# An eight-core decoder step: a second u buffer, the layer-norm weight in PSUM and late gating matmuls in place of a bf16 start of FFN 0

## The reference, cut to what matters

```
layer 0: x += 0.5 * swiglu(rmsnorm(x));  x += even_mixer(rmsnorm(x));  x += 0.5 * swiglu(rmsnorm(x))
layer 1: x += 0.5 * swiglu(rmsnorm(x));  x += odd_mixer(rmsnorm(x));   x += 0.5 * swiglu(rmsnorm(x))
y = rmsnorm(x)
rmsnorm(x)   = x * rsqrt(mean(x*x) + 1e-6) * g
swiglu(h)    = (silu(h @ w_gate) * (h @ w_up)) @ w_down            # width 2816
even_mixer:  uv = gelu(h @ w_in[:, :1024]);  u = uv[:512]
             v  = layernorm(uv[512:]) * ln_g + ln_b
             y_a = u * (tril(w_s) . v + b_s)                       # per head, in chunks of 128 tokens
             y_b = gate_b * conv3(gate_c * x_in)                   # three more projections of h
             out = [y_a, y_b] @ w_out
```

## Time and profile before

| what | value |
|---|---|
| median of the runs | 2394.33 us |
| lowest run, which is the profiled one | 2394.22 us |
| its span, first to last instruction, slowest core (5) | 2392.7 us |
| spans of the eight cores | 2362.3 to 2392.7 us |
| TensorE busy | 2329.3 us, 97% |
| VectorE / ScalarE / GpSimd busy | 1014.0 / 546.3 / 216.3 us |

### The profile page before, as it was taken

The page is one execution under the profiler, slowest core; times in us unless marked ns, Lnnn a source line. Parts: engine busy times, 40 slices in busy tenths (PEclk is TensorE's granted clock), DMA queues, the critical chain, the costliest instruction groups (busy, mean ns, idle before and its releaser), DMA issues.

```text
span 2392.7 us, 33520 instructions; the slowest of 8 cores (2362.3 to 2392.7 us)
## 1 busy us (share of the span) xinstructions
PE 2329.3 (97%) x12456; PEld 1225.2 (51%) x12456; DVE 1014.0 (42%) x1717; ACT 546.3 (23%) x992; POOL 216.3 (9%) x261
## 2 busy tenths in 40 slices
PE   6999999998999999999999999999989999999996
PEld 3455555554555555555555555555544555555553
DVE  4752232276567242232382422322796624223226
ACT  4401101254234101101242011012433310110123
POOL 2100000165000000000000000001500000000014
PEclk9999999999999999999999999999998899999998
DMA  8052222210422132222220522222231113222203
GB/s 225 18 84 36 36 36 36 36 20 13 68 41 32 25 60 36 36 36 36 36 32 5 80 36 36 36 36 36 49 72 21 32 24 61 36 36 36 36 1 150
DMA packets 21326, 107.38 MB, mean 45 GB/s; under 512 B 4016, under 2 KB 6064, under 8 KB 11696
## 3 DMA queue, kind: packets, MB, share of 16 engines
q0 software_dynamic: 12528, 84.42, 22.5%
q1 hardware_dynamic: 8640, 20.82, 2.6%
HBM read 174.89 MB, written 11.08 MB: 78 GB/s over the span
## 4 chain that ended last, share of the span: by engine, by line
PE 91%; DVE 4%; issue 2%; ACT 1%; DMA 1%; POOL 1%; DVEq 0%; ACTq 0%; SPq 0%; POOLq 0%
PE ps L436 88%; PE ps L431 2%; DVE hT L665 1%; PE ps L724 1%; DVE scr L1153 0%; PE ps L608 0%; DVE xT L653 0%; DVE xT L820 0%; DMA ws<-wall 0%; DVE hT L653 0%; DVE misc L898 0%; POOL mid L948 0%; DMA xT<-x 0%; ACT scr L916 0%; DMA scr<-spl 0%
## 5 line engine op out<-in xcount | busy, mean ns | idle before, releaser
L436 PE MATMUL ps<-hT,ws 128*128 128x512 bf16 (+2 forms) x7520 | 1403.2, 350 | 3.0 <-ACT mid L1131 2.2
L436 PEld LDWEIGHTS ps<-hT,ws 128*128 128x128 bf16 x7520 | 738.2, 98 | 660.9 <-issue 38.8
L436 PE MATMUL ps<-mid,ws 128*128 128x512 bf16 (+2 forms) x4160 | 783.8, 351 | 0.0
L713 DVE TENSOR_TENSOR mid<-ps,scr 128x512 bf16<-128x512 f32 (+2 forms) x428 | 261.4, 611 | 921.3 <-PE ps L436 886.0
L436 PEld LDWEIGHTS ps<-mid,ws 128*128 128x128 bf16 x4160 | 408.2, 99 | 368.5 <-issue 34.1
L708 ACT ACTIVATE scr<-ps 128x512 f32<-128x512 f32 (+2 forms) x428 | 227.5, 532 | 1405.8 <-PE ps L436 1335.2
L820 DVE SCALAR_TENSOR_TENSOR xT<-ps,xT 128x512 f32<-128x512 f32 (+2 forms) x480 | 290.0, 611 | 284.2 <-PE ps L436 283.6
L386 POOL DMA_DIRECT2D ws<-wall x83 | 44.4, 535 | 1954.3 <-PE ps L436 1936.4
L665 DVE SCALAR_TENSOR_TENSOR hT<-xT,misc,nrm 128x512 bf16<-128x512 f32 (+2 forms) x144 | 91.6, 677 | 4.4 <-ACT nrm L635 4.4
L431 PE MATMUL ps<-hT,ws 128*128 128x512 bf16 (+2 forms) x288 | 60.6, 365 | 2.9 <-DVE hT L665 2.9
L1061 DVE TENSOR_TENSOR xT<-ps,xT 128x512 f32<-128x512 f32 (+2 forms) x80 | 48.6, 610 | 34.6 <-PE ps L436 33.4
(11 more groups left out here) (108 smaller groups left out, 644.7 us busy)
## 6 DMA issues: line engine op xcount, KB each, us to landing
ws<-wall POOLq DMA_DIRECT2D x65, 1024.0 KB, 9.5
ws<-wall POOLq DMA_DIRECT2D x12, 768.0 KB, 8.9
y<-xT SPq DMA_DIRECT2D x4, 1024.0 KB, 3.9
xT<-x SPq DMA_DIRECT2D x6, 512.0 KB, 7.0
ws<-wall POOLq DMA_DIRECT2D x6, 512.0 KB, 16.8
xT<-x POOLq DMA_DIRECT2D x2, 1024.0 KB, 24.0
xT<-x SPq DMA_DIRECT2D x2, 1024.0 KB, 8.1
y<-xT SPq DMA_DIRECT2D x4, 512.0 KB, 2.7
```

What stands on the lines that cost most here:

```text
L436: ins = e.matmul(banks[bk][:, 0:n], l, rr, start=(i == 0), stop=(i == len(pairs) - 1))
L713: P.add("dve", lambda e: e.tensor_tensor(out=mcol(fs, a, a + n), in0=banks[ku][:, 0:n], in1=s_(0, n), op=ALU.mult), r=[("ps", ku), s_.key( ...
```

## The change

The bf16 start goes: `start`, `raw`, `raw_out`, `raw_in`, `direct`, `quad`, `line`, `rs0` and `finish_h`. Block 0 is normed chunk by chunk (eight groups; chunks 1, 3 and 6 of h by GpSimd and ScalarE), all its h are listed, and the cells start with block 0; block 1's norm is listed after the third cell, with its ones-matmul ahead of the fourth. x comes in 1 MB pieces on SyncE's queue: block 0 at once, block 1 after the second half of the first weight item, each later one after the block before. The six weight pieces follow each other on GpSimd's queue. Blocks 1 and 2 change sizes, to 512 and 384.

In the even mixer u has two buffers, by turns; `lngb` is copied by ScalarE into bank 7 once block 1 begins, after all h of the last block, and `center` reads it there from then on; the last two `sgu` stand behind the three groups of the first convolution cell, and so do the memset of `ext` and the state's DMA. The `xin` buffers move to the norm's scratch.

```diff
-BL = [(0, 512), (512, 384), (896, 512), (1408, 512), (1920, 256)]
-XPER = [2, 4, 4, 4, 4]
+BL = [(0, 512), (512, 512), (1024, 384), (1408, 512), (1920, 256)]
...
-    uT = R.f32(6 * T * 2, 4 * 512)
+    uTs = [R.f32(6 * T * 2, 4 * 512), NRM.f32(0, 4 * 512)]
...
-    xin = [SC.f32(2048 * i, 512) for i in range(2)]
+    xin = [NRM.f32(8192 + 2048 * i, 512) for i in range(2)]
...
-        for lo, hi in [part] if part else [(0, n)]:
+        pieces = [(0, 2048), (2048, 4096)] if j < 3 else [(0, n)]
+        for lo, hi in pieces:
...
                 P.label = "v norm"
-                P.add("dve", lambda e: e.scalar_tensor_tensor(out=g(0, 512), in0=g(0, 512), scalar=mv(2 * i, 2 * i + 1), in1=lngb(0, 512),
+                gain, gk = (banks[7][:], ("rsp",)) if gain7 else (lngb(0, 512), lngb.key(0, 512))
+                P.add("dve", lambda e: e.scalar_tensor_tensor(out=g(0, 512), in0=g(0, 512), scalar=mv(2 * i, 2 * i + 1), in1=gain,
...
             ensure_h(b)
+            if b == 1:
+                ensure_h(NB - 1)
+                P.label = "v norm"
+                P.add("act", lambda e: e.activation(out=banks[7][:], in_=lngb(0, 512), func=AF.Copy), r=[lngb.key(0, 512)], w=[("ps", 7), ("rsp",)])
+                gain7.append(1)
...
+            uT = uTs[b % 2]
             for j in range(4):
...
             prev = [(i, b) for i in tiles]
-        while prev:
-            sgu(*prev.pop(0))
         release(jv)
         release(ju)
...
                     mm_group(bk, n, [(wt(o + c * 128, o + c * 128 + 128), hs(b, c)) for c in range(NCH)],
                              [hk(b, c) for c in range(NCH)] + [wt.key(o, o + 1024)])
+                while prev:
+                    sgu(*prev.pop(0))
...
+                if cn["k"] == 1:
+                    P.add("sp", lambda e: [e.dma_start(out=exs(0, 640), in_=sc_in)], w=[exs.key(0, 640)], ndma=1)
+                    P.add("dve", lambda e: e.memset(ext(0, 2), 0.0), w=[ext.key(0, 2)])
...
-    for c in range(0, NCH, 2):
-        load_x("sp", 0, c)
-    load_item(0, (0, 2048), [xT.key(0, 1)])
-    load_item(0, (2048, 4096))
-    load_item(1, (0, 2048))
-    load_x("pool", 1, 0)
-    load_x("pool", 1, 4)
-    load_item(1, (2048, 4096))
-    load_x("pool", 2, 0)
-    load_x("pool", 2, 4)
-    load_item(2, (0, 2048))
-    load_item(2, (2048, 4096))
...
+    load_item(0, after=[xT.key(0, 1)])
+    load_item(1)
+    load_item(2)
+    for b in range(1, NB):
+        gate = wv(0).key(2048, 4096) if b == 1 else xT.key(xoff(b - 1, 4), xoff(b - 1, 4) + 1)
         for c in (0, 4):
-            load_x("sp", b, c, [gate])
+            load_x(b, c, [gate])
     nm0 = Norm(0)
+    nm0.groups[0] = 8
+    nm0.split[0] = (1, 3, 6)
+    nm0.pair_wait = 2
...
-        nm0.wait = 5
+        nm0.wait = 3 if b < 2 else 5
...
+    norm0(0)
+    ensure_h(0)
...
-    cells = [(2, 0, 3), first(3)] + [(2, f, 3) for f in range(1, 5)] + [finish_h(0), (2, 5, 3), first(4), lambda: load_item(3)] \
-        + [(3, f, 3) for f in range(4)] + [finish_h(1)] + [(3, f, 3) for f in range(4, 6)] + [(4, f, 3) for f in range(6)] + [even_consts, odd_consts]
+    cells = [(0, 0), (0, 1), (0, 2), first(1), (0, 3, 8), (1, 0), first(2), (1, 1), (1, 2), (1, 3), (0, 4), (1, 4),
+             first(3), (2, 0), (2, 1), (2, 2), (2, 3), (2, 4), (0, 5), (1, 5), (2, 5), first(4), lambda: load_item(3),
+             (3, 0), (3, 1), (3, 2), (3, 3), (3, 4), (3, 5)] + [(4, f) for f in range(6)] + [even_consts, odd_consts]
```

More of the change, by code:

```diff
@@ L317, in xdram @@
     def xdram(b, c0, c1):
-        return dram(x_in, b, c0, c1, XPER[b])
+        return dram(x_in, b, c0, c1, 4)
     def ydram(b, c0, c1):
@@ L368, in build_program, with load_item @@
     slot_of = {}
-    def load_item(j, part=None, after=()):
+    def load_item(j, after=()):
         key, n = ITEMS[j]
@@ L538, in heavy_chunk @@
             if i == end:
[L539 to L579, removed]
+                at(2 if alone else 5, lambda: self.stat(b, k, 0, 2 if alone else 1))
         def prescale(self, b, c):
@@ L594, in flush, with stat @@
                 self.scaled = None
-        def stat(self, b, k, gi, groups=None, own=False):
+        def stat(self, b, k, gi, groups=None):
             n = BL[b][1]
             bk, rk = 7, ("rsp",)
-            if own:
+            if groups == 2:
                 if gi == 0:
@@ L611, in stat @@
                 return
[L612 to L619, removed]
+            k2 = pc["rs"] % 2
+            pc["rs"] += 1
+            q = rs[k2]
+            while any(x[2] == k2 for x in hq):
+                hq.pop(0)[1]()
             P.label = f"norm{self.nidx} rs"
@@ L714, in gu @@
                   r=[("ps", ku), s_.key(0, n)], w=[mkey(fs, a, a + n)])
[L716 to L803, removed]
-                tick(3)
-                if b * 10 + f in (3, 12):
-                    for c in range(0, 4) if f == 3 else range(4, 8):
-                        nm0.line(2, c)
-            o[2]()
@@ L835, in ffn @@
                 js = [item(("gu", l, w, f)) for f in fs]
-                js0.extend(js)
-                if cells is not None:
-                    start()
                 if cells is None:
@@ L967, in even @@
                          [hk(b, c) for c in range(NCH)] + [wu_.key(j * 1024, j * 1024 + 1024)])
-                P.add("act", lambda e, j=j, bk=bk, n=n: e.activation(out=uT(j * 512, j * 512 + n), in_=banks[bk][:, 0:n], func=AF.Gelu),
+                P.add("act", lambda e, j=j, bk=bk, n=n, uT=uT: e.activation(out=uT(j * 512, j * 512 + n), in_=banks[bk][:, 0:n], func=AF.Gelu),
                       r=[("ps", bk)], w=[uT.key(j * 512, j * 512 + n)])
@@ L978, in even @@
         P.label = "conv init"
-        P.add("dve", lambda e: e.memset(ext(0, 2), 0.0), w=[ext.key(0, 2)])
-        P.add("sp", lambda e: [e.dma_start(out=exs(0, 640), in_=sc_in)], w=[exs.key(0, 640)], ndma=1)
         cn = dict(k=0)
@@ L1222, in build_program, with load_x, norm0 @@
     P.add("act", lambda e: e.activation(out=junk(0, 1), in_=mh(0, 1), func=AF.Square), r=[("mh",)], w=[("junk",)])
-    def load_x(eng, b, c, gate=()):
-        o0, o1 = xoff(b, c), xoff(b, c) + XPER[b] * BL[b][1]
+    def load_x(b, c, gate=()):
+        o0, o1 = xoff(b, c), xoff(b, c) + 4 * BL[b][1]
         P.label = "load x"
-        P.add(eng, lambda e: [e.dma_start(out=xT(o0, o1), in_=xdram(b, c, c + XPER[b]))], r=list(gate), w=[xT.key(o0, o1)], ndma=1)
+        P.add("sp", lambda e: [e.dma_start(out=xT(o0, o1), in_=xdram(b, c, c + 4))], r=list(gate), w=[xT.key(o0, o1)], ndma=1)
+    load_x(0, 0)
+    load_x(0, 4)
     P.label = "const"
     P.add("sp", lambda e: [e.dma_start(out=cT(0, 76), in_=cst)], w=[("cT",)], ndma=1)
-    for c in range(0, NCH, 2):
-        load_x("sp", 0, c)
-    load_item(0, (0, 2048), [xT.key(0, 1)])
-    load_item(0, (2048, 4096))
-    load_item(1, (0, 2048))
-    load_x("pool", 1, 0)
-    load_x("pool", 1, 4)
-    load_item(1, (2048, 4096))
-    load_x("pool", 2, 0)
-    load_x("pool", 2, 4)
-    load_item(2, (0, 2048))
-    load_item(2, (2048, 4096))
-    for b in range(3, NB):
-        gate = wv(2).key(0, 2048) if b == 3 else xT.key(xoff(b - 1, 4), xoff(b - 1, 4) + 1)
+    load_item(0, after=[xT.key(0, 1)])
[3 more added lines that the diff above has]
+        gate = wv(0).key(2048, 4096) if b == 1 else xT.key(xoff(b - 1, 4), xoff(b - 1, 4) + 1)
         for c in (0, 4):
-            load_x("sp", b, c, [gate])
+            load_x(b, c, [gate])
     nm0 = Norm(0)
+    nm0.groups[0] = 8
+    nm0.split[0] = (1, 3, 6)
+    nm0.pair_wait = 2
     cur_norm[0] = nm0
-    def nm0_block(b):
-        nm0.wait = 5
+    def norm0(b):
+        nm0.wait = 3 if b < 2 else 5
         for c in range(NCH):
@@ L1370, in to_blocks @@
     x3 = xt.reshape(NCH, 128, T)
-    return np.concatenate([x3[c:c + p, :, a:a + n].transpose(1, 0, 2).reshape(-1) for (a, n), p in zip(BL, XPER) for c in range(0, NCH, p)])
+    return np.concatenate([x3[c:c + 4, :, a:a + n].transpose(1, 0, 2).reshape(-1) for a, n in BL for c in (0, 4)])
 def from_blocks(y):
```

15 lines of the change are left out of this document (5 added, 10 removed).

## The result

The changed kernel takes 2367.28 us, the one before took 2394.27 beside it: ratio 0.9891, interval [0.9869, 0.9914]. That is 27 us faster where 8 were forecast; the time lies in the range of the prediction (2356 to 2399) and outside the likeliest case's own (2379 to 2392). Left out of every comparison and count here, unless one is named, are the runs in which one die took over 1% longer than the other at a lower clock, or which took over 1.5% longer than the fastest of their kernel.

The account below looks back on a forecast made before the run. TensorE, busy 2329 of 2392.7 us, was taken as the bound, with core 5 setting the time. From 2394.2, 7.8 us for gating and 0.5 for the start gave 2385.9, say 2386; range 2356 to 2399.

Parts of the forecast that it names:

- the likeliest case: Whole kernel: both edits win as summed and the slow stretch stays; 2386 us, own range 2379 to 2392, chance 0.58.
- Gating, what goes: Gating stage: TensorE's 5.9 us of waits and 1.9 us of half clock vanish; 7.8 us, bounds 4.8 to 7.8.
- Gating, what is added: Gating stage: centring from PSUM at 0.69 us, copy to PSUM, moved memset and DMAs; all put at nothing.
- The bank named as next to be late: Second convolution cell's third bank: freed 2 us after the gating matmuls, TensorE comes to it after 3.5 us.
- The clock: Gating stage: with no pause, granted clock stays 1.00 through its end, saving 1.9 us.
- Start, steps 1 to 4: Start: block 0's x, first weights, block 0's norm and cells 1 and 2, ending at 32.7 us.
- Step 3's rule: Block 0's norm: shared port fully blocking would make the h 7.6 us, not 5.7, and the start 1.9 us later.
- Step 5: Start, block 1's norm: TensorE waits from 32.7 to 39.7 us for VectorE's seven adds.
- the third case: Block 1's x behind the weights: lands at 37.6, ones-matmul at 41.7 us; part of the late-start rival, 2390 us, chance 0.13.
- The stretch: Core 5 at clock 0.81 from 1780 to 1940 us: not edited, so taken to stay, change nothing.
- The other rival: The 0.81 stretch grows as the load gets denser; twice as long gives 2416 us; chance 0.08.
- the rival of the lost stretch: Core 5 keeps its clock after 1780 us and gains 28 us: 2358 us; chance 0.10.

Follow-up runs that it names:

- e4: Kernel before (old bf16 start) with the new gating stage and the sample's v stored from its own tile; 2359.9 us without the stretch.
- e3: Changed kernel with the sample's v stored from a tile of its own; 2359.7, 2360.2 and 2360.6 us without the stretch.
- e12: e3 with the last gating matmuls ahead of the convolution matmuls again; first down matmul to end 2232.3 to 2234.0 us on spared cores.
- e10: e3 with one u buffer again; first down matmul to end 2229.1 to 2230.0 us on spared cores.
- e6: e3 with five more VectorE passes ahead of the first convolution product, an equal delay on every core; 2367.76 us.
- e2: Changed kernel with the gating stage of the kernel before; ratio 0.9943, 2368.2 to 2369.7 us without the stretch.
- e5: Changed kernel run again unaltered, on a chip without the stretch; 2367.36 us, ratio 0.9993.
- e9: Changed kernel run a third time unaltered, on a chip that shows the stretch; ratio 0.9928.
- e8: e3 with block 1's x gated on the first half of the first weight item; 2358.79 us, ratio 0.9956.

## Why the prediction was right, and where it was wrong

- *Gating, what goes.* Right in kind: both waits are gone, the centring takes 0.74 (0.69 taken). Its size was 7.8 with 7.8 as the upper bound; 7.9 was there with the old blocks (e4) and 8.8 with the new ones (e3). Its cause was half right: with both the u buffer and the weight in PSUM but the matmuls in their old place, 2.64 us of wait are left (e12), and with the matmuls late enough ScalarE may stand as before (e10).
- *Gating, what is added.* The step that failed, and it ate most of the gain: "The DMAs of the third and fourth convolution weights now stand on GpSimd's queue ahead of the last two gating multiplies", "All at nothing". It asked who on GpSimd's queue waits for these loads, and not which transfer shares the DMA engines with them. The store of v then took 11.3 us instead of 3.0, its source is overwritten by the first convolution product, and with the half clock that is 6.0 to 6.5 us on the slowest core. The bank named as next to be late, the second cell's third, was in time. TensorE waits two groups later, at the third cell's second group, for the bank that the first product frees behind two GpSimd products, a ScalarE pass and two VectorE passes: 0.33 us in e3, where 1.5 to spare ("3.5 us" against "2 us") had been worked out for the other bank.
- *The clock.* The forecast of "granted clock 1.00 through the end of the gating stage" was wrong for the same cause: 0.53 from 606 to 612. A pause there costs over one and a half times its length (6.0 us for 3.4 on core 7, 6.4 for 4.0 in e6).
- *Start, steps 1 to 4.* Right: first half of x 9.0 (9.3 predicted), h from 16.1 (16.0), third cell's end 32.8 (32.7).
- *Step 3's rule.* Five h took 6.54 us, last h 22.7 instead of 21.9; the row had given 5.7. VectorE lost 6.54 - 3.45 = 3.1 us beside 4.68 us of GpSimd multiplies, two thirds. The Trainium skill, "SBUF — State Buffer", section "Who interferes with whom", makes the shared port an exclusive lock, by which the prediction estimated 7.6; full exclusion isn't what the trace shows.
- *Step 5.* Equal shares were taken; on four of eight cores, the slowest among them, the third case came: x at 37.6 predicted, 38.0 seen, ones-matmul 41.7 and 42.2. The slowest first down matmul came at 128.8 instead of 125.4, inside the bounds (121 to 130) and 2.9 us behind the 125.9 of the profile before. But the old start can be as late: in e4 its slowest core has 128.1. By the times of the runs (e2 against before) the start is worth nothing, where -0.5 was put.
- *The stretch.* This term made the result. It was kept at 0.58 because "nothing that leads to it is edited"; its price, 28 us by core 6, is 23 to 24 by the medians of whole runs on one chip (2392.7 with it and 2369.1 without; 2392.7 and 2369.9). The mistake was to read one profile's stretch as a trait of the kernel. It is an event of single runs and of pairs of cores, and the edit did change the distance between them. The other rival, that a denser load makes it grow, found nothing in any run. The Trainium skill, "TensorE: Matmul & The Clock Gate", section "Seeing it yourself", tells of a die-wide limiter; what is described here struck pairs.

In sum: the edits were put at -8.3 and gave -2 to -3 (e5; e9's 2366.9 against 2369.9 without the stretch), the stretch was put at nothing and gave the rest, some -24. The time lies in the range only because the range took in the rival of the lost stretch, which had a chance of 0.10; for the likeliest case, at 0.58, that is luck. The rival's own sum, 2358, missed by 9 us: what the edits lacked and the smaller price of the stretch.

## What to carry to other kernels

Here a load moved ahead in one queue slowed the store issued just behind it on another, from 3.0 to 11.3 us: for each transfer behind such a load, look who overwrites its source or reads its target next. Price a pause of TensorE with the half clock behind it: 4.3 us of waiting cost 6.4 here. And before a clock stretch is taken as fixed or as gone, count it over many runs, cores and chips; the two mends of e8, worth 0.44% against the kernel before with the stretch in neither, were not run on a chip that has it, and e3, one half of them, shows it there.

## Unexpected on the hardware

- A stretch of 0.81 strikes neighbouring cores two by two (0 and 1, 2 and 3, 4 and 5, 6 and 7), costs a pair 20 to 30 us, ends under full load, and can come in the start as well as in the odd stage. On one chip it came in none of 59 runs.
- A kernel with a needless wait beats the same kernel without it on chips with the stretch: 2367 against 2380 to 2385 in the runs struck, while it loses by 7 us where the stretch stays away.
- A store of 256 KB issued 0.8 us behind 1.5 MB of weight loads lands with them, after 11.3 us; issued 3 us ahead of them it takes 3.0, and 2.1 to 2.3 in e12.
